# A two-stack block on one core: the context's norm and queries between the stacks, and layer 0's attention with values four items behind

## The reference

```python
        h = rmsnorm(x, g_ple_pre[i])
        e = jax.nn.sigmoid(h @ w_ple_gate[i]) * (p[i].astype(x.dtype) @ w_ple_proj[i])
        x = x + rmsnorm(e, g_ple_post[i])
```

```python
        h = _modulate(_rmsnorm(x, norm1_g[i]), sh1, sc1)
        hc = _modulate(_rmsnorm(xc, norm1_g[i]), shc1, scc1)
...
    q, k, v = _project(h, w_qkv, splits)
    qc, kc, vc = _project(hc, w_qkv, splits)
...
    s = jnp.einsum('bqhmd,bkhmd->bhmqk', q, k).astype(jnp.float32) / math.sqrt(q.shape[-1])
    p = jax.nn.softmax(s, axis=-1)
    a = p[:, :, 0] - lam * p[:, :, 1]
    return jnp.einsum('bhqk,bkhd->bqhd', a.astype(v.dtype), v)
...
        o = _rmsnorm(o, subln_g) * (1.0 - lam_init)
```

## Time and profile before

| what | us |
|---|---|
| median of 3 runs | 3017.91 (3016.14 to 3020.22) |
| the profiled execution | 3016.83 |
| its span | 3015.6 |
| PE busy in the span | 2670.6 (89%) |
| DVE, ACT, POOL busy | 751.3, 483.6, 212.8 |
| mean granted TensorE clock | 0.963 of full |
| the chain that ended last | PE 76%, DMA 12%, DVE 5%, ACT 3%, issue 3% |

### The profile page before, as it was taken

How to read it: one execution, slowest core, us unless ns; L and a number is a source line. 1 busy time by engine, 2 the same in 40 slices (tenths; PEclk the granted TensorE clock), 3 DMA queues, 4 the chain that set the end, 5 groups by cost and what they waited for, 6 DMA issues and landing times.

```text
span 3015.6 us, 57462 instructions
## 1 busy us (share of the span) xinstructions
PE 2670.6 (89%) x24534; PEld 1982.5 (66%) x24534; DVE 751.3 (25%) x2039; ACT 483.6 (16%) x1182; POOL 212.8 (7%) x392
## 2 busy tenths in 40 slices
PE   8999999999999999997998899988776998776676
PEld 7888788887888778885444456665555466544444
DVE  2002520023002430014116621211113163332323
ACT  2001310011001220003104521110002151000001
POOL 1001010011001010001000012221211000000000
PEclk9999999999999999998999999999988999999999
DMA  7553465546453455542320039999996314999997
GB/s 265 179 171 112 157 239 173 174 157 223 153 192 111 162 202 203 195 157 106 144 84 29 3 144 375 411 411 421 420 420 236 105 52 179 420 419 419 419 419 296
DMA packets 251832, 690.23 MB, mean 229 GB/s; under 512 B 15247, under 2 KB 142942, under 8 KB 235230
## 3 DMA queue, kind: packets, MB, share of 16 engines
q1 hardware_dynamic: 240352, 675.27, 59.0%
q0 software_dynamic: 7552, 10.76, 1.0%
q10 hardware_dynamic: 3710, 0.99, 0.1%
HBM read 669.95 MB, written 17.04 MB: 228 GB/s over the span
## 4 chain that ended last, share of the span: by engine, by line
PE 76%; DMA 12%; DVE 5%; issue 3%; ACT 3%; SPq 0%; ACTq 0%; POOL 0%; POOLq 0%; DVEq 0%
PE ps L663 18%; DMA arena<-in_moe_w_up 11%; PE ps L674 10%; PE ps L1443 5%; PE ps L2287 5%; PE ps L2262 3%; PE ps L2790 3%; PE ps L2302 3%; PE ps L1497 2%; PE ps L894 2%; PE ps L687 2%; PE ps L1054 2%; PE ps L2042 2%; PE ps L2751 1%; PE ps L2814 1%
## 5 line engine op out<-in xcount | busy, mean ns | idle before, releaser
L663 PE MATMUL ps<-arena 128*128 128x256 f32 x2560 | 568.6, 379 | 3.5 <-DVE arena L745 3.5
L663 PEld LDWEIGHTS ps<-arena 128*128 128x128 f32 x2560 | 483.0, 189 | 73.8 <-issue 4.1
L674 PE MATMUL ps<-arena 128*128 128x256 f32 x1408 | 318.0, 379 | 0.0
L674 PEld LDWEIGHTS ps<-arena 128*128 128x128 f32 x1408 | 264.9, 189 | 46.1 <-issue 8.4
L2287 PE MATMUL ps<-arena 128*32 128x128 f32 x6016 | 193.6, 286 | 61.1 <-issue 58.6
L2287 PEld LDWEIGHTS ps<-arena 128*32 128x32 f32 x6016 | 177.6, 115 | 71.9 <-issue 67.6
L2790 PE MATMUL ps<-arena 128*32 128x128 f32 x4096 | 138.7, 294 | 82.3 <-issue 80.6
L787 DVE TENSOR_TENSOR arena<-arena,ps 128x256 f32<-128x256 f32 x76 | 32.1, 422 | 638.4 <-ACT arena L755 633.7
L2790 PEld LDWEIGHTS ps<-arena 128*32 128x32 f32 x4096 | 125.5, 118 | 90.0 <-issue 89.0
L1443 PE MATMUL ps<-arena 128*128 128x512 f32 (+1 forms) x384 | 162.6, 601 | 5.6 <-ACT arena L1390 5.6
L755 ACT ACTIVATE arena<-ps 128x256 f32<-128x256 f32 x76 | 29.2, 384 | 675.1 <-PE ps L663 675.1
(11 more groups left out here) (457 smaller groups left out, 3091.6 us busy)
## 6 DMA issues: line engine op xcount, KB each, us to landing
arena<-in_moe_w_gate SPq DMA_DIRECT2D x64, 2048.0 KB, 24.8
arena<-in_moe_w_up SPq DMA_DIRECT2D x64, 2048.0 KB, 25.5
arena<-in_moe_w_down SPq DMA_DIRECT2D x64, 2048.0 KB, 30.4
arena<-in_mod_w SPq DMA_DIRECT2D x24, 2048.0 KB, 13.0
arena<-in_w_gate SPq DMA_DIRECT2D x44, 1024.0 KB, 5.3
arena<-in_w_up SPq DMA_DIRECT2D x44, 1024.0 KB, 7.9
arena<-in_w_down SPq DMA_DIRECT2D x44, 1024.0 KB, 4.8
arena<-in_w_in SPq DMA_DIRECT2D x12, 1024.0 KB, 6.0
```

Of the source, the lines that this page charges most:

```text
L663: last = pe.matmul(k.ps[:, T % 4, off:off + S], w[:, t, T % 2 * P:(T % 2 + 1) * P], h[:, t, :], start=(t == 0), stop=(t == KT - 1), skip_g ...
L674: last = pe.matmul(acc[:, t, :], d[:, T % 2, t * P:(t + 1) * P], k.hid[:, T % 4, :], start=(T == 0 and t % 2 == 0), stop=end, skip_group_c ...
```

## The change

Two parts. First, the context's share of the start of the second stack is taken out of it. POOL squares and adds the context's tiles in layer 1's second feed-forward part; PE sums them there with one matmul ahead of the last down product, and ACT takes the root behind that part's post-norm. In the ple part of layer 1 DVE makes the context's reciprocal and scaled tiles behind its second scaling, and ACT shifts them between its second and third sigmoid. PE projects the context's queries from them in eight tiles of 256 columns: 0 and 1 ahead of the post-norm's sums, 2 to 5 behind them, 6 and 7 behind the sums of x. The two blocks of query weights go to the memory of K and V, and SP issues them and the constants in the ple part. The norm of x works on 256 columns, each square behind its own addition, and the query projection that stays has 256 columns.

Second, attention in layer 0. The value product is of item n - 4 in place of n - 3. The factor 0.125 moves from the exponentials into the queries, so the maxima are negated by their own reduction. The maps are joined by one operation, map 1 times (sum 0 x lambda / sum 1) plus map 0, behind a factor of one column; the division by sum 0 is made where the product is copied out. Squares are made for two items at once on ACT and summed by a DVE reduction.

The diff, cut to its core:

```diff
@@ pe_ffn, act_ffn (layer 1, second part) @@
+    if (l, f) == (1, 1):
+        pe_context_sum(k)
     down(2 * CHUNKS - 1)
...
     act_post_norm(k, l, f"ffn{f}", k.banks(4, 4, S), ends)
+    if (l, f) == (1, 1):
+        act_context_root(k)
@@ act_post_norm @@
+    if (l, name) == (1, "ple"):
+        act_context_queries(k, (0, 1))
     act.wait_ge(*s["post_summed"].at(l, name))
@@ sp_ple @@
+    else:
+        sp.wait_ge(*s["mod_product"].at(l, 11))
+        sp_query_weights(k, 0)
     sp.wait_ge(*s["ple_product"].at(l, "up", 3))
     quarter(3)
+    if l == 1:
+        sp_query_weights(k, 1)
+        sp.wait_ge(*s["zeroed"].at(1, D // 2))
+        sp.wait_ge(*s["ple_product"].at(l, "gate", 2))
+        sp.dma_start(*k.const2).then_inc(*s["const2"].up())
@@ pe_ple, act_ple, dve_ple @@
     quarter(3, k.h)
+    if l == 1:
+        pe_context_queries(k, (0, 1))
     pe_post_norm(k, l, "ple")
...
         act.activation(e, src, ACT.Sigmoid).then_inc(*s["ple_gated"].up(l, b))
+        if (l, b) == (1, 1):
+            act_context_shifts(k)
...
+    if l == 1:
+        dve_modulated(k, "a0", 0, 0, (1,))
     for b in range(4):
@@ new functions (also act_context_root, act_context_shifts, act_context_queries) @@
+CONTEXT_BANKS = (1, 2, 3, 4, 5, 6, 1, 2)
+def pool_context_squares(k):
+    pool, s = k.nc.gpsimd, k.s
+    pool.wait_ge(*s["added"].at(1, "mix", KT - 1))
+    for t in range(KT):
+        pool.tensor_tensor(k.csq[:, t, :], k.x[:, t, S:2 * S], k.x[:, t, S:2 * S], ALU.mult).then_inc(*s["c_squares"].up(t))
+        if t > 0:
+            pool.wait_ge(*s["c_squares"].last())
+            pool.tensor_tensor(k.csq[:, 0, :], k.csq[:, 0, :], k.csq[:, t, :], ALU.add).then_inc(*s["c_squares"].up(t, "added"))
+def pe_context_queries(k, tiles):
+    pe, s = k.nc.tensor, k.s
+    free = [s["ple_scaled"].at(1, 1), s["ple_gated"].at(1, 2), s["ple_gated"].at(1, 3), s["ple_done"].at(1, 0), s["ple_done"].at(1, 1), s["ple_done"].at(1, 2),
+            s["c_out"].at(0), s["c_out"].at(1)]
+    for j in tiles:
+        if j % 4 == 0:
+            pe.wait_ge(*s[f"slot{j // 4}"].at("chunk", j // 4))
+        if j == 0:
+            pe.wait_ge(*s["t_made"].at("a0", KT - 1, 1))
+        pe.wait_ge(*free[j])
+        for t in range(KT):
+            last = pe.matmul(k.ps[:, CONTEXT_BANKS[j], 0:S], k.qweights[j // 4][:, t, j % 4 * P:(j % 4 + 1) * P], k.h2[:, t, S:2 * S],
+                             start=(t == 0), stop=(t == KT - 1), skip_group_check=True)
+        last.then_inc(*s["c_tile"].up(j))
@@ pe_project @@
+        if not slots and j == 1:
+            pe.wait_ge(*s["c_out"].at(7))
@@ pe_program, act_program @@
+    pe_context_queries(k, (2, 3, 4, 5))
     for t in range(KT):
-        pe_sums(k, "a0", t, 2 * S)
+        pe_sums(k, "a0", t)
+    pe_context_queries(k, (6, 7))
     pe.wait_ge(*s["const2"].at())
-    pe_project(k, "q0", 0, (0, 1), 2 * S, 8, made=[s["t_made"].at("a0", t, 1) for t in range(KT)])
+    pe_project(k, "q0", 0, None, S, 8, made=[s["t_made"].at("a0", t, 0) for t in range(KT)])
...
     for t in range(KT):
-        act_square(k, "a0", t, 2 * S)
-    act_modulated(k, "a0", 0, 0, (0, 1))
-    act_project(k, "q0", k.Q, 2 * S, 8)
+        act.wait_ge(*s["added"].at(1, "ple", t))
+        act_square(k, "a0", t)
+    act_context_queries(k, (2, 3, 4, 5))
+    act_modulated(k, "a0", 0, 0, (0,))
+    act_context_queries(k, (6, 7))
+    act_project(k, "q0", k.Q, S, 8)
@@ pe_attend @@
-    for n in range(N + 3):
+    N, maps, behind = len(items), 2 if l else 1, 3 if l else 4
+    for n in range(N + behind):
...
-        i = n - 3
+        i = n - behind
@@ dve_attend_a @@
-            V.tensor_reduce(st[:, 0:2], ps[:, 2 * (n % 2):2 * (n % 2) + 2, 0:nk], AX, ALU.max).then_inc(*step.up())
-            V.wait_ge(*step.last())
-            V.tensor_scalar(st[:, 2:4], st[:, 0:2], -0.125, None, ALU.mult).then_inc(*step.up(0, n))
+            V.tensor_reduce(stats(k, n)[:, 0:2], ps[:, 2 * (n % 2):2 * (n % 2) + 2, 0:nk], AX, ALU.max, negate=True).then_inc(*step.up(0, n))
...
-            V.tensor_scalar(pr[:, 1, :], pr[:, 1, :], st[:, 7:8], k.lam[:, 2:3], ALU.mult, ALU.mult).then_inc(*step.up())
+            V.scalar_tensor_tensor(st[:, 8:9], st[:, 4:5], k.lam[:, 2:3], st[:, 7:8], ALU.mult, ALU.mult).then_inc(*step.up())
             V.wait_ge(*step.last())
-            V.scalar_tensor_tensor(pr[:, 0, :], pr[:, 0, :], st[:, 6:7], pr[:, 1, :], ALU.mult, ALU.add).then_inc(*s["wt_dve"].up(0, i))
-        i = n - 3
+            V.scalar_tensor_tensor(pr[:, 0, :], pr[:, 1, :], st[:, 8:9], pr[:, 0, :], ALU.mult, ALU.add).then_inc(*s["wt_dve"].up(0, i))
+        i = n - 4
...
-            V.tensor_copy(rows_of(k)[:, t, q * P:(q + 1) * P], ps[:, 6 + i % 2, 0:P]).then_inc(*s["av_out_dve"].up(0, i))
+            V.tensor_scalar(rows_of(k)[:, t, q * P:(q + 1) * P], ps[:, 6 + i % 2, 0:P], stats(k, i)[:, 6:7], None, ALU.mult).then_inc(*s["av_out_dve"].up(0, i))
+        i = n - 6
+        if i >= 0 and i % 2:
+            V.wait_ge(*s["av_squared"].at(0, i))
+            V.tensor_reduce(k.ss.rearrange("p (t h) -> p t h", t=4)[:, t - 1:t + 1, q:q + 1], two_blocks(k.rscale2), AX, ALU.add).then_inc(*s["av_summed"].up(0, i))
```

More of the change, by code:

```diff
@@ L1258, in sp_ple, with sp_query_weights @@
         sp_modulation(k, l, 11)
+    else:
+        sp.wait_ge(*s["mod_product"].at(l, 11))
+        sp_query_weights(k, 0)
     sp.wait_ge(*s["ple_product"].at(l, "up", 3))
     quarter(3)
+    if l == 1:
[3 more added lines that the diff above has]
+        sp.dma_start(*k.const2).then_inc(*s["const2"].up())
+def sp_query_weights(k, i):
+    sp, s = k.nc.sync, k.s
+    sp.dma_start(k.qweights[i], columns(k.a["a_w_qkv_2"][0], 512 * i)).then_inc(*s[f"slot{i}"].up("chunk", i))
 def pe_ple(k, l):
@@ new lines, in pe_context_sum, with act_context_root @@
+def pe_context_sum(k):
+    pe, s = k.nc.tensor, k.s
+    pe.wait_ge(*s["c_squares"].at(KT - 1, "added"))
+    pe.matmul(k.ps[:, 0, S:2 * S], k.c["ones"], k.csq[:, 0, :], start=True, stop=True, skip_group_check=True).then_inc(*s["c_summed"].up())
+def act_context_root(k):
+    act, s = k.nc.scalar, k.s
+    act.wait_ge(*s["zeroed"].at(1, D // 2))
+    act.wait_ge(*s["c_summed"].at())
+    act.activation(k.at[:, 0, S:2 * S], k.ps[:, 0, S:2 * S], ACT.Sqrt, scale=1.0 / D, bias=k.eps[:, 0:1]).then_inc(*s["t_root"].up("a0", 1))
@@ new lines, in act_context_shifts @@
+def act_context_shifts(k):
+    act, s = k.nc.scalar, k.s
+    for t in range(KT):
+        H = k.h2[:, t, S:2 * S]
+        act.wait_ge(*s["t_normed"].at("a0", t, 1))
+        act.activation(H, H, ACT.Identity, bias=k.mod_col(0, 0, t, 1)).then_inc(*s["t_made"].up("a0", t, 1))
+def pe_context_queries(k, tiles):
+    pe, s = k.nc.tensor, k.s
+    free = [s["ple_scaled"].at(1, 1), s["ple_gated"].at(1, 2), s["ple_gated"].at(1, 3), s["ple_done"].at(1, 0), s["ple_done"].at(1, 1), s["ple_done"].at(1, 2),
[6 more added lines that the diff above has]
+        pe.wait_ge(*free[j])
+        for t in range(KT):
+            last = pe.matmul(k.ps[:, CONTEXT_BANKS[j], 0:S], k.qweights[j // 4][:, t, j % 4 * P:(j % 4 + 1) * P], k.h2[:, t, S:2 * S],
+                             start=(t == 0), stop=(t == KT - 1), skip_group_check=True)
+        last.then_inc(*s["c_tile"].up(j))
@@ L1342, in streams_of, with act_context_queries @@
+def act_context_queries(k, tiles):
+    act, s = k.nc.scalar, k.s
+    for j in tiles:
+        act.wait_ge(*s["c_tile"].at(j))
+        act.activation(k.Q[:, j, S:2 * S], k.ps[:, CONTEXT_BANKS[j], 0:S], ACT.Copy, scale=factor_of("q0")).then_inc(*s["c_out"].up(j))
 def streams_of(l, which):
@@ L1428, in pe_project @@
     for j in range(tiles):
[L1429 to L1432, removed]
+        w = chunk_view(k, slots[j // 4], n) if slots else k.qweights[j // 4]
+        if slots and j % 4 == 0:
+            pe.wait_ge(*s[f"slot{slots[j // 4]}"].at("chunk", first + j // 4))
+        if not slots and j == 1:
+            pe.wait_ge(*s["c_out"].at(7))
         if j >= 4:
@@ L1619, in act_attend_a @@
     N = len(items)
-    for n in range(N + 4):
+    for n in range(N + 5):
         if n < N:
             nk = items[n][4]
-            st, pr = k.st[:, n % 4, :], probs(k, n, nk)
+            st, pr = stats(k, n), probs(k, n, nk)
             act.wait_ge(*s["sc_dve"].at(0, n))
@@ L2971, in sp_program @@
     sp.wait_ge(*s["added"].at(1, "ple", KT - 1))
-    sp.wait_ge(*s["zeroed"].at(1, D // 2))
-    sp.dma_start(*k.const2).then_inc(*s["const2"].up())
     a = k.a
     w = a["a_w_qkv_2"][0]
-    for n in range(6):
+    for n in range(2, 6):
         sp_chunk(k, n, n, columns(w, 512 * n))
@@ L3116, in pool_program @@
         pool_prepare(k, l, "ffn1", added_before(k, l, "mix"))
+        if l == 1:
+            pool_context_squares(k)
         pool_prepare(k, l, "ple", added_before(k, l, "ffn1"))
```

67 lines of the change are left out of this document (34 added, 33 removed).

## The result

| | median us | range | ratio [95%] |
|---|---|---|---|
| before | 3017.86 | 3016.14 to 3020.22 | |
| after | 2970.99 | 2968.11 to 2971.64 | 0.9842 [0.9825, 0.9859] |

Each median is that of four executions. The predicted 2971.5 is 0.5 us off. The steps are what counts. The profiled execution took 2971.54 us, with a span of 2970.3.

What follows compares the result with a forecast made beforehand. TensorE bounds most of the kernel, but the stack boundary and layer 0's attention are chains of waits. 3016.83 - 28.3 - 18 = 2970.5, plus 1.1 from profiled execution to median, given as 2971.5; range 2966 to 2980, with two rivals 2963 to 2987.

Steps and rivals of the forecast that it cites:

- Part 1: Boundary between the stacks: context's norm and queries move to where TensorE stood; 28.3 us saved, bounds 25 to 29.5.
- The order on TensorE: Boundary: order followed from quarter 3's end at 1396.58; queries of x at 1430.0, keys at 1461.5 instead of 1489.76.
- the post-norm's sums: Boundary: four sums behind context tiles 0 and 1 run at the upper clock, 1.7 us instead of 3.51.
- The contention with GpSimd: ffn1: GpSimd's 15 operations delay two VectorE products; 1.2 us allowed, hidden by later slack, cost 0, at worst 1.
- Quarter 3, issued later: Gate stage: weight quarter issued at 1382.70, due half at 1389.6; landing in 4.8 to 7.4 us, cost taken as 0.
- Part 2: Layer 0's attention: distance of four removes the value product's wait, engines' own work decides; 18 us saved, bounds 8 to 21.
- The head: Attention head period falls from 11.03 to 8.8 us, from VectorE work of 8.5 and TensorE's 8.36; saving 17.8.
- The stage's ends and dips: Attention stage: value products no longer pile up at the end, -1 us; clock dips cost more, +1 us.
- A new wait in attention: Rival, attention: a new wait keeps the head at 10 to 11 us; time 2981 to 2989, middle 2985; chance 0.13.
- Part 1 lost in part: Rival, boundary: late weight transfer or post-norm behind context tiles; 14 us lost if four tiles lengthen the path, 2985; chance 0.04.
- The expert stage swallowing the gain: Rival, experts: weight transfers don't move up, so the end doesn't either; time 3018; chance 0.02.
- The slower clock: Rival, attention: TensorE's denser work stays at 1.2 GHz, 16.7 us a head; time 3026; chance 0.02.

Runs made afterwards that it cites:

- e6: The changed kernel with all eight context query tiles put behind the sums of x; 2984.7 us, ratio 0.9890.
- e1: The changed kernel with the old kernel's attention functions, so only the boundary part is changed; 2992.3 us, ratio 0.9906.
- e2: The old kernel with only the attention part of the change and the scaled queries; 3001.9 us, ratio 0.9944.
- e4: e1 with only the value product's distance changed, to four items behind, old attention operations kept; 2977.9 us, ratio 0.9864.
- e5: The changed kernel with ScalarE squaring one item at a time and accumulating the sums, no VectorE reduction for them; 2965.2 us, ratio 0.9820.
- before_again: The old kernel, unedited, run once more for a second trace; 3019.7 us.
- after_again: The whole changed kernel, unedited, measured a second time; 2973.2 us, ratio 0.9848.
- e3: The changed kernel with the value product and its output again three items behind, new operations kept; 2980.4 us, ratio 0.9872.

## Why the prediction was right

The two mechanisms came as forecast, and the total came near by luck. In the profiled pair the two stretches gave 30.5 + 21.4 = 51.9 us, 5.6 more than the 28.3 + 18 of the sum. Code outside them gave 6.6 back: the first gate matmul of the boundary came 3.1 later (1359.9 for 1356.8; the sum had 0.4 of it), and the rest took 3.5 more. 45.3 is left.

**Part 1, predicted 28.3.** Part 1's stretch is 190.6 to 191.7 without it (four traces) and 161.1 to 162.7 with it (seven, e6 aside). Both spreads have one source, the third step below; compared like with like the gain is 28.9 to 29.6. The sum's 28.3 holds a loss of 0.43 for the context's sum, which lies ahead of this stretch, so 28.7 stands against it. The steps:
- The order on TensorE came out as forecast. Counted from the end of quarter 3, the first query matmul of x starts 32.9 us later (1430.92 - 1398.05); predicted were 33.0 (1430.0 - 1397.0). The keys start 64.3 later; predicted 64.5. In absolute time both came 0.9 late, since that quarter ended 1.05 later than I had it. The first gate matmul of the boundary starts at 1356.8 to 1359.1 in four traces without part 1 and at 1356.0 to 1359.9 in eight with it, so code ahead of it scatters by more than that.
- That the post-norm's sums would run at 2.4 GHz when TensorE isn't idle ahead of them was right: 1.73 for the predicted 1.7.
- A term that I left out: the projection of p, ahead of quarters 2 and 3, took 8.71 us in before at a mean clock of 0.80 and 7.03 in after at 1.00, the same 32 records. It is the slower one in five traces (before, e1, e2, e4, e5) and the faster in seven, before_again among them, so it is a gain of 1.7 in this comparison and not one of the change: e1, with the same part 1, has 162.7, after 161.1.
- The contention with GpSimd was hidden, as allowed for: VectorE's two products took 3.21 beside GpSimd's squares, 2.36 before, 0.85 more of an allowance of 1.2.

```profile
1124.91 3.21 DVE L584 TENSOR_TENSOR arena<-arena 128x1024 f32<-128x1024 f32 x2
```

In the chain TensorE's run of 32 records beside them took 7.04 us as before, and the next (1131.30) followed without a gap.

- Quarter 3, issued later, landed in time: no wait stands ahead of L1294's second half, whose 64 records take 13.86 for 13.88.

**Part 2, predicted 18, measured 21.4 in the profiled pair** (107.4 to 86.0; 19.2 with after_again's 88.2, 20.8 in e2). The mechanism was right, the wait for the copy gone and VectorE the bound. Two terms were mis-sized, and they offset in part.
- The head: 9.08, not 8.8. VectorE's durations per form:

```profile
L1691 DVE TENSOR_REDUCE arena<-ps 128x2 f32<-128x1024 f32 x10 | 12.2, 1215 | 0.0
L1701 DVE SCALAR_TENSOR_TENSOR arena<-arena 128x512 f32<-128x512 f32 x10 | 7.5, 753 | 0.4
L1706 DVE TENSOR_SCALAR arena<-ps,arena 128x128 f32<-128x128 f32 x20 | 6.9, 345 | 0.0
...
L1699 DVE SCALAR_TENSOR_TENSOR arena<-arena 128x1 f32<-128x1 f32 x20 | 4.4, 219 | 0.7
```

  The one-column factor is 219 ns, not the reciprocal's 160, and the output with a scalar from memory 345, not the copy's 285: 4 x 0.06 + 4 x 0.06 = 0.48. Recorded durations sum to 9.97 a head (reductions 3.79, join 2.48, output 1.38, factor 0.88, sums 0.82, reciprocals 0.62), and the period is 0.89 less. The timeline (start, us, engine, line) shows why:

```profile
1604.13 1.22 DVE L1691 TENSOR_REDUCE arena<-ps 128x2 f32<-128x1024 f32 x1
1605.26 0.16 DVE L1697 RECIPROCAL arena<-arena 128x2 f32<-128x2 f32 x1
1605.45 0.22 DVE L1699 SCALAR_TENSOR_TENSOR arena<-arena 128x1 f32<-128x1 f32 x1
1605.71 0.48 DVE L1701 SCALAR_TENSOR_TENSOR arena<-arena 128x256 f32<-128x256 f32 x1
1606.11 0.34 DVE L1706 TENSOR_SCALAR arena<-ps,arena 128x128 f32<-128x128 f32 x1
```

  The reciprocal starts 0.09 before the reduction's recorded end, the output 0.08 before the join's; the factor, which waits for the reciprocal, starts 0.03 behind its end, the join 0.04 behind the factor's. So 9.97 - 14 x 0.085 + 8 x 0.035 = 9.06: the overlap taken from the earlier trace rows holds, and the two durations were the error of the VectorE sum (9.06 for 8.5). I had then added 0.3 for two engines that feed each other; the period is VectorE's sum within 0.02, so that allowance was wrong too, and hid half of the first error.
- The stage's ends and dips: eight heads save 8 x (11.03 - 9.08) = 15.6, so 5.8 of the 21.4 lie outside steady heads. I had put 0 there. Before, the stage was 97.4 against 8 x 11.03 = 88.2, so 9.2 over; after, 75.7 against 72.7, 3.0 over. The starts of the reductions divide it. Two heads of before had a dip (12.09 for 11.03), none of after: 2.1. The first two heads of after took 8.01 and 8.89, below its own 9.08, where the first of before took 11.60: 1.8. From the last head's first reduction to the output projection it is 22.5 for 26.3, 1.9 beyond a head's own saving. The mean clock rose with it, 0.91 to 0.98. I expected dips to cost more with TensorE nearly full; they cost less here. They are not gone for good: in after_again the first two heads took 8.89 and 10.36, and that is the 2.2 by which its stage is longer.

The Trainium skill, "VectorE: DVE Perf Modes", section "The DRAIN you can't avoid", says that the next operation does not start until the pipe of the one before is empty, and that a semaphore between two costs nothing extra. Read as the prediction read it, that makes the period the sum of recorded durations, 9.97, and the gain of the steady heads 8 x (11.03 - 9.97) = 8.5; the chain shows 9.08, and the trace does not agree. The same section adds that an operation that is not held starts earlier, which the prediction passed over and the trace bears out (0.08 to 0.09 here). On the semaphore the trace differs: an operation that waits starts 0.03 to 0.04 behind the recorded end, one that need not 0.08 to 0.09 ahead of it, so the wait costs about 0.12 us.

**The rivals.** A new wait in attention: none; the head of e3, 10.50, is what that rival would have looked like, with the old wait in place. Part 1 lost in part: the unbroken chain at the boundary shows that it did not occur. That e6, 2984.7, lands on its 2985 is chance: the rival had four tiles lengthen the path, and e6 moves six of them, 20.8 us of work, for 13.0 us of time. The expert stage swallowing the gain: no, the rest grew by 3.5 us, which unchanged code does by itself. The slower clock: attention's clock rose.

**What I had not priced** was the scatter of untouched code. It took back 6.6 of 51.9 us in the profiled pair and decides how near the number came.

## What to carry to other kernels

When a chain of small operations crosses engines, find which wait holds the busiest engine's queue; one item more of distance removed a wait that shorter operations alone didn't (e3 against e4), and in a steady head the shorter operations then gave 0.95 us in place of 0.53. The whole stage need not show this, since its ends and dips are as large. Work that depends on nothing nearby is worth most where TensorE would idle: in e6 the idle time also doubled the time of the next sums, 3.80 for 1.73. Before a few us in untouched code are given a cause, take a second trace of the old kernel.

## What was not expected of the hardware

- GpSimd and VectorE delay each other both ways: beside VectorE's two products of 128x1024, GpSimd's operations of 128x256 took 1.59 in place of 0.61 or 0.73.

```profile
1125.45 1.59 POOL L1381 TENSOR_TENSOR arena<-arena 128x256 f32<-128x256 f32 x1
...
1128.67 0.73 POOL L1381 TENSOR_TENSOR arena<-arena 128x256 f32<-128x256 f32 x1
```

  Alone, the two products (2.36) and the three GpSimd operations beside them (0.61, 0.73, 0.61) are 4.31 us; together they took 3.82 (1124.76 to 1128.58). So little of it ran side by side, as far as GpSimd's rough spans can tell.

- A VectorE operation on one column takes 219 ns with two tensors and a scalar read from memory, and the reciprocal of two columns 156; at such sizes the kind of operation counted for more than the columns.
- Two executions of one kernel differ by up to 12 us of 2970 (after_again: 2964.8 to 2977.1), 0.4%. In the traces, the same code from the output projection on took 1303.7 to 1311.1 us.
